# The stage ahead of the latent attentions: a rope moved across a stage boundary, keys of two heads in one product, an early exponential table, an output by banks

## The reference, cut to what matters

```
h = x normed, times w_in_2        -> q, k_cmp, v_cmp, k_sel, v_sel, k_win, v_win, gates, cq, ckv, kr
sparse attention: k_cmp, v_cmp compressed by a small MLP to 31 blocks (silu);
  softmax over the blocks, over the selected and over the window keys, summed with the gates
latent attention: q = norm(cq) w_q_up, [k, v] = norm(ckv) w_kv_up, kr shared by 8 heads
x = x + [sparse, latent] w_out ;  x = x + relu(norm(x) w_ff1)^2 w_ff2
```

## Time and profile before

| what | value |
|---|---|
| time, 3 runs | median 2813.57 us (2811.67 to 2826.16) |
| profiled execution, own time | 2809.47 us |
| its span | 2807.7 us |
| mean granted PE clock over the span | 0.961 |
| PE busy | 2617.4 us (93% of the span) |
| prepare stage, first layer | PE from 1530.03 to 1583.21 us |
| prepare stage, second layer | PE from 2206.19 to 2259.21 us |

### The profile page before, as it was taken

The page is one execution under the profiler, slowest core; times in us unless marked ns, Lnnn a source line. Parts: engine busy times, 40 slices in busy tenths (PEclk is TensorE's granted clock), DMA queues, the critical chain, the costliest instruction groups (busy, mean ns, idle before and its releaser), DMA issues. The chain is left out here.

```text
span 2807.7 us, 56794 instructions
## 1 busy us (share of the span) xinstructions
PE 2617.4 (93%) x21851; PEld 1768.2 (63%) x21852; DVE 1350.4 (48%) x2758; ACT 747.9 (27%) x1650; POOL 301.1 (11%) x449
## 2 busy tenths in 40 slices
PE   6999889899988889998979999999999999999998
PEld 6977774344433333443457567888888666888887
DVE  3246645344433434454465675533344576543333
ACT  4235430000000000000032565422233256433222
POOL 4121002122222112222210000000000000000000
PEclk8999999999999999999989999999999999999999
DMA  7353169999999999899973201222223300122221
GB/s 226 87 210 116 76 261 380 420 418 405 419 420 403 419 419 411 340 418 419 416 267 101 91 2 37 91 91 98 90 101 91 112 31 1 68 91 98 90 95 56
DMA packets 170890, 588.47 MB, mean 210 GB/s; under 512 B 28238, under 2 KB 55694, under 8 KB 121512
## 3 DMA queue, kind: packets, MB, share of 16 engines
q1 hardware_dynamic: 158112, 562.91, 51.2%
q0 software_dynamic: 10192, 18.09, 1.9%
q10 hardware_dynamic: 2360, 4.29, 0.4%
HBM read 573.54 MB, written 17.45 MB: 210 GB/s over the span
## 5 line engine op out<-in xcount | busy, mean ns | idle before, releaser
L2774 PE MATMUL moe_up<-expert_w,mod 128*32 128x512 f32 x3200 | 395.2, 620 | 52.5 <-DMA expert_w<-in_exp_w_up 26.7
L2774 PEld LDWEIGHTS moe_up<-expert_w,mod 128*32 128x32 f32 x3200 | 114.2, 112 | 283.4 <-issue 213.5
L2839 ACT ACTIVATE mod<-mod 128x256 f32<-128x256 f32 x85 | 35.5, 417 | 965.2 <-DVE mod L2875 956.4
L2774 PE MATMUL moe_up<-ring,mod 128*32 128x512 f32 x1784 | 219.3, 612 | 26.8 <-DMA ring<-in_exp_w_up 20.5
L423 ACT ACTIVATE feed_w<-ring 128x1024 fp32r<-128x1024 f32 (+1 forms) x160 | 153.8, 1035 | 263.5 <-PE feed_bank L370 263.5
L2783 PE MATMUL moe_down<-expert_w,mod 128*32 128x256 f32 x3568 | 216.5, 386 | 1.7 <-DVE mod L2886 1.7
L368 PE MATMUL feed_bank<-feed_w,mlp_u_hi 128*128 128x512 f32 x512 | 199.3, 389 | 0.0
L370 PE MATMUL feed_bank<-feed_w,mlp_u_lo 128*128 128x512 f32 x512 | 199.2, 389 | 0.0
L369 PE MATMUL feed_bank<-feed_w,mlp_u_hi 128*128 128x512 f32 x512 | 199.2, 389 | 0.0
L2783 PEld LDWEIGHTS moe_down<-expert_w,mod 128*32 128x32 f32 x3568 | 132.6, 112 | 96.4 <-issue 42.1
L437 DVE TENSOR_TENSOR feed_w<-ring,feed_w 128x1024 fp32r<-128x1024 f32 (+1 forms) x160 | 185.4, 1221 | 13.2 <-ACT feed_w L423 12.9
(11 more groups left out here) (556 smaller groups left out, 5035.3 us busy)
## 6 DMA issues: line engine op xcount, KB each, us to landing
expert_w<-in_exp_w_up SPq DMA_DIRECT2D x153, 1024.0 KB, 10.4
expert_w<-in_exp_w_down SPq DMA_DIRECT2D x83, 1024.0 KB, 10.3
ring<-in_exp_w_up SPq DMA_DIRECT2D x80, 1024.0 KB, 10.4
ring<-in_w_ff SPq DMA_DIRECT2D x32, 2048.0 KB, 8.8
ring<-in_exp_w_down SPq DMA_DIRECT2D x32, 1024.0 KB, 10.2
ring<-in_ada_w SPq DMA_DIRECT2D x12, 2048.0 KB, 10.5
x<-in_exp_w_up SPq DMA_DIRECT2D x23, 1024.0 KB, 10.3
x<-in_exp_w_down SPq DMA_DIRECT2D x13, 1024.0 KB, 10.0
```

The costliest lines, as they stand in the source:

```text
L2774: mm = nc.tensor.matmul(up[quarter[q], :], rowsT[:, c, :], w[:, q], start=(c == 0), stop=(c == UPS - 1))
L2839: nc.scalar.activation(sig, gate, ACT.Sigmoid, scale=ALPHA).then_inc(sig_ready, 1)
```

## The change

- Rope of the keys: tiles 0 and 1 after job 13 as before, tile 2 after job 14 (when ACT has copied job 14), tile 3 no longer in the projection's stage: its four instructions stand at the head of DVE's list in the prepare stage, with `rot[:, 0]` as room, and PE waits for the last of them ahead of the transposes of `k_cmp`.
- Key columns of all heads first, then the value columns, in `w_kv_up_2` (set in order on the host ahead of the launch). A key up now makes two heads in one product with 128 weight columns: 4 key ups in place of 8, 16 ups in all. Each is copied out by two copies of 64 partitions.
- An exponential of one column (`warm`) right after the silu on ACT.
- `ov` is laid out so that a bank holds one group and two tiles; PE signals after each bank, and DVE multiplies bank by bank, four instructions in place of two.

```diff
-        if n in (13, 15):
-            dve.wait_ge(self.evac_done["act"], self.before["act"] + (n + 1) // 2)
-            dve.wait_ge(self.evac_done["dve"], self.before["dve"] + (n + 1) // 2)
-            for t in (n - 13, n - 12):
+        if n in (13, 14):
+            dve.wait_ge(self.evac_done["act"], self.before["act"] + n // 2 + 1)
+            dve.wait_ge(self.evac_done["dve"], self.before["dve"] + 7)
+            for t in {13: (0, 1), 14: (2,)}[n]:
...
+        warm = sb("warm", [P, 1])
...
-        ov = ctx.enter_context(nc.psum_tensor(f"prep{l}_o", [P, NT, COL], F32))
+        ov = ctx.enter_context(nc.psum_tensor(f"prep{l}_o", [P, 2 * G2, 2, 256], F32))
...
-        wv = wkv[:, 0, :].rearrange("p (h n) -> p h n", n=DN + DV2)[:, :, DN:]
+        wv = wkv[:, 0, H2 * DN:]
...
-        ups = [("q", *j) for j in UPQ] + [("v", t) for t in range(NT)] + [("k", h) for h in range(H2)]
+        ups = [("q", *j) for j in UPQ] + [("v", t) for t in range(NT)] + [("k", h) for h in range(0, H2, 2)]
...
-                    c = job[1] * (DN + DV2)
-                    mm = nc.tensor.matmul(out[:DN, :], wkv[:, 0, c:c + DN], lat[:, 2, :], start=True, stop=True)
+                    mm = nc.tensor.matmul(out, wkv[:, 0, job[1] * DN:(job[1] + 2) * DN], lat[:, 2, :], start=True, stop=True)
...
             pe.wait_ge(lat_dve, 1)
+            pe.wait_ge(key_added, 1)
             turn(bank[1], columns_of(tok, KC, P)).then_inc(kc_turned, 1)
...
-            for n in range(12, 15):
+            for n in range(12, 14):
...
-            for n in range(15, 20):
+            for n in range(14, 16):
...
-                    pe.wait_ge((up_act, up_dve)[h % 2], 9 + h // 2)
+                    pe.wait_ge((up_act, up_dve)[h % 2], 7 + h // 2)
...
-                    mm = nc.tensor.matmul(ov[:, t, g * 256:(g + 1) * 256], pT[:, g, t * P:(t + 1) * P], vbd[:, g, :], start=True, stop=True)
-                mm.then_inc(valued, 1)
+                    mm = nc.tensor.matmul(ov[:, 2 * g + t // 2, t % 2, :], pT[:, g, t * P:(t + 1) * P], vbd[:, g, :], start=True, stop=True)
+                    if t % 2:
+                        mm.then_inc(valued, 1)
...
+            return [(mkT[0:DN, job[1] + m, :], src[m * DN:(m + 1) * DN, :]) for m in range(2)]
...
             nc.scalar.activation(hid[:], bank[0][:, 0:CHID], ACT.Silu).then_inc(activated, 1)
-            for n in (8, 10, 12, 14):
+            nc.scalar.activation(warm[:], k.eps[:], ACT.Exp)
+            for n in (8, 10, 12):
                 take_up(n)
...
-            for n in (16, 18):
-                take_up(n)
+            take_up(14)
...
+            nc.vector.tensor_tensor(other[..., 0:w], keys[..., w:], ksin[..., 0:w], ALU.mult).then_inc(key_turned, 1)
+            nc.vector.tensor_tensor(other[..., w:], keys[..., 0:w], ksin[..., w:], ALU.mult).then_inc(key_turned, 1)
+            dve.wait_ge(key_turned, 2)
+            nc.vector.tensor_tensor(keys, keys, kcos, ALU.mult).then_inc(key_turned, 1)
+            dve.wait_ge(key_turned, 3)
+            nc.vector.tensor_tensor(keys, keys, other, ALU.add).then_inc(key_added, 1)
             dve.wait_ge(lat_turned, 2)
...
-            dve.wait_ge(valued, G2)
-            for g in range(G2):
+            for b in range(2 * G2):
+                g, ts = b // 2, slice(b % 2 * 2, b % 2 * 2 + 2)
+                dve.wait_ge(valued, b + 1)
```

More of the change, by code:

```diff
@@ L3140, in prepare_stage @@
         paired, placed = sem("paired"), sem("placed")
+        key_turned, key_added = sem("key_turned"), sem("key_added")
         kr_turned, kr_spread = sem("kr_turned"), sem("kr_spread")
@@ L3147, in prepare_stage @@
             sem(t) for t in ("biased", "shifted", "raised", "weighed", "ca_turned", "ca_taken", "valued", "step"))
-        ov = ctx.enter_context(nc.psum_tensor(f"prep{l}_o", [P, NT, COL], F32))
+        ov = ctx.enter_context(nc.psum_tensor(f"prep{l}_o", [P, 2 * G2, 2, 256], F32))
         low = [ctx.enter_context(nc.psum_tensor(f"prep{l}_bank{i}", [P, COL], F32)) for i in range(4)]
-        bank = [b[:] for b in low] + [ov[:, t, :] for t in range(NT)]
+        bank = [b[:] for b in low] + [ov[:, b].rearrange("p t n -> p (t n)") for b in range(2 * G2)]
         w1 = [chunk_view(k, ("cmp", l, kv))[0] for kv in "kv"]
         wq, wkv = chunk_view(k, ("up", l))
-        wv = wkv[:, 0, :].rearrange("p (h n) -> p h n", n=DN + DV2)[:, :, DN:]
+        wv = wkv[:, 0, H2 * DN:]
         block = ctx.enter_context(nc.Block())
@@ L3277, in up_out @@
             if job[0] == "q":
-                return tok[:, job[1], job[2]:job[3]], src[:, 0:job[3] - job[2]]
-            return (mv[:, job[1], :], src) if job[0] == "v" else (mkT[0:DN, job[1], :], src[:DN, :])
+                return [(tok[:, job[1], job[2]:job[3]], src[:, 0:job[3] - job[2]])]
+            if job[0] == "v":
+                return [(mv[:, job[1], :], src)]
+            return [(mkT[0:DN, job[1] + m, :], src[m * DN:(m + 1) * DN, :]) for m in range(2)]
         @block.scalar
@@ L3284, in take_up @@
                 act.wait_ge(upped, n + 1)
-                nc.scalar.activation(*up_out(n), ACT.Copy).then_inc(up_act, 1)
+                for dst, src in up_out(n):
+                    copied = nc.scalar.activation(dst, src, ACT.Copy)
+                copied.then_inc(up_act, 1)
             for i, gain in ((0, k.q_norm[:, l, 0:1]), (2, k.kv_norm[:, l, :])):
@@ L3336, in take_up @@
                 dve.wait_ge(upped, n + 1)
-                nc.vector.tensor_copy(*up_out(n)).then_inc(up_dve, 1)
+                for dst, src in up_out(n):
+                    copied = nc.vector.tensor_copy(dst, src)
+                copied.then_inc(up_dve, 1)
             def pair_up(i, b, turns):
@@ L3372, in _ @@
             dve.wait_ge(up_dve, 4)
+            dve.wait_ge(key_added, 1)
             nc.vector.tensor_tensor(rot[:, :, :, 0:DR // 2], q[:, :, :, DR // 2:], sn[:, :, :, 0:DR // 2], ALU.mult).then_inc(rot_turned, 1)
@@ L3393, in _ @@
                     nc.vector.tensor_copy(vbd[32 * r:32 * r + 32, g, 64 * r:64 * r + 64], bank[g][32 * r:32 * r + 32, 0:DK2]).then_inc(vbd_made, 1)
-            for n in (15, 17, 19):
-                take_up(n)
+            take_up(15)
             dve.wait_ge(k.groups_done, up_done)
@@ L3720, with keys_then_values @@
           "w_q_up_2 mla_kv_norm_2 w_kv_up_2 nsa_out_norm_2 mla_out_norm_2 w_out_2 mlp_norm_2 w_ff1_2 w_ff2_2 final_norm_2").split()
+def keys_then_values(w):
+    heads = w.reshape(*w.shape[:2], H2, DN + DV2)
+    return np.ascontiguousarray(np.concatenate([heads[..., c].reshape(*w.shape[:2], -1) for c in (slice(0, DN), slice(DN, None))], axis=-1))
 def kernel(**inputs):
@@ L3728 @@
     arrays = {n: np.ascontiguousarray(inputs[n]) for n in INPUTS}
+    arrays["w_kv_up_2"] = keys_then_values(arrays["w_kv_up_2"])
     arrays |= {f"const_{n}": v for n, v in host_constants().items()}
```

9 lines of the change are left out of this document (6 added, 3 removed).

## The result

The changed kernel takes 2784.62 us (median of 4 runs, 2783.47 to 2788.04), the kernel before in 4 runs 2812.62 us (2805.29 to 2826.16): ratio 0.9897, with a 95% interval of 0.9858 to 0.9936. The forecast was 2787.5 us, faster, range 2780 to 2799.

A forecast was written before the change was run, and what follows sets the result against it. PE was taken as the bound in the dense stretch, with DVE, ACT and a halved clock costing time at the stage's edges. Six terms sum to 13.05 us a layer, 26.1 for two: 2787.5 us as median, range 2780 to 2799.

The forecast's parts named there:

- 1. Rope: Projection's end to prepare stage: with the turns moved, SP arrives last and PE begins earlier, saving 2.7 us a layer.
- 2. The clock behind it: Start of the prepare stage: the clock stays up, so 28 transposes take 0.109 us each instead of 0.211; 2.8 us a layer.
- the nearest row: Profile row from 1575 to 1579 us: PE had a 1.46 us gap and the clock stayed at 1.00.
- the clock falls at the first boundary too: Rival, both boundaries at low clock: gain only 8.65 us a layer, 2796.3 us in all; chance 0.12.
- The thin cover of 0.4 us for `kv_up`: Before the ups: `kv_up` lands at 1531.7 us, PE asks for the up weights at 1532.1.
- late weights: Rival at the ups: small loads served before `kv_up` make PE wait 1.7 us a layer, 2790.9 us; chance 0.05.
- 3. Keys of two heads: Key ups in the prepare stage: four products fewer, eight records at 0.434 us, save 3.5 us a layer of full PE.
- 4. The table: Load before the exponential moves behind silu, so the mask begins earlier: 0.8 us a layer, bounds 0 and 1.28.
- 5. Output by banks: End of the prepare stage: only one 0.69 us multiplication of 2.35 remains behind PE's last bank; 1.65 us a layer.
- 6. The clock in the attention: Attention's start: idle time falls from 2.77 to 1.1 us, the clock stays up; 1.6 us a layer, bounds 0 and 2.4.
- the largest rival (0.30): Attention's start stays at half clock: gain 11.45 us a layer, 2790.7 us in all; chance 0.30.
- The side "slower": Clock stays low beyond the transposes, in the always-busy stretch from 1536 to 1572 us; 2832 us if all slow; chance 0.02.

The follow-up runs named there:

- table alone: Only the one-column exponential behind silu, put on the kernel before; one execution, 2805.01 us beside 2805.86.
- rope alone: Only the moves of tile 2's and tile 3's key rope, put on the kernel before; one execution, 2797.49 us beside 2809.68.
- the kernels whose gaps were filled: Unread PE products added in idle time: kernel before with 24 and 14, 2802.77 us; with 11 and 6, 2799.5; changed kernel with fills, 2781.06.

## Why the prediction was right, point by point

**1. Rope, 2.7 us: right.** 2.71 measured (2.65 in the second layer), with SP's drain the last to arrive. No cover was used up: the rope of tile 3 ends at 1529.68 and the copy behind it at 1530.34, 2.5 and 1.9 us ahead of the transposes that need them.

**2. The clock behind it, 2.8 us: right, and the nearest row was the right one.** 2.82 in the first layer, 2.66 in the second. The rival "the clock falls at the first boundary too" did not happen in any of 10 stages with a gap of 1.35 us. The bound behind it was near, though: at 2.61 and 2.56 us it fell, twice out of twice. The length of one gap would not have been enough everywhere: at the attention's end, behind gaps of 1.61, 1.03 and 2.01 us close together, the clock falls. The thin cover of 0.4 us for `kv_up` held; PE goes from its transposes to the ups without a wait, although the small loads issued behind the boundary landed after 3.9 to 4.5 us instead of 2.1: the part of the rival "late weights" that was true, but it reached no waiting instruction. The transfers issued from 1525 to 1536 us in the changed kernel (KB, us to landing):

```profile
prep_w2k<-in_cmp_w_k SPq DMA_DIRECT2D x2, 64.0 KB, 4.5
prep_w2v<-in_cmp_w_v SPq DMA_DIRECT2D x1, 64.0 KB, 3.9
```

**3. Keys of two heads, 3.5 us: the mechanism was right, the term too small by 0.4.** 3.87 measured, in every kernel that has the edit. The sixteen records of the key ups took 2.72 + 4.44 = 7.16 us up to what follows them, 0.4475 each, so eight fewer are 3.58; the 0.434 of the working runs from the first start to the last and leaves out the step behind the last record. The other 0.29 us the working had as unchanged: 0.2 in the small products between and 0.1 in the step to the first key up. No cover failed.

**4. The table, 0.8 us: right.** 0.80 and 0.80 alone. The Trainium skill, ScalarE: Activation LUTs, What ACT_TABLE_LOAD costs, gives some 1.38 us of drain behind the load, and the trace again does not agree: from the end of the load at 1552.82 the next ACTIVATE takes 0.01 us to begin, and PE's way to the scores did not grow by the 0.3 us that would follow (12.49 us with the table alone).

**5. Output by banks, 1.65 us: right in size, 1.74, but by a thinner cover than I said.** The one piece of 0.69 us behind PE's last bank is what was taken; the inverse sums, however, were ready only at 1571.76, 0.6 us behind the first bank, and three multiplications of together 2.04 us stand between them and the last one. Of the 2.2 us up to the end of the last bank 0.17 were left, where the working had 1.2 to spare. Later by more than that, and the term would have begun to shrink.

**6. The clock in the attention, 1.6 us: right.** 1.67 and 1.65. This was the term with the largest rival (0.30). With 1.03 us of gap the clock stayed up in all 12 stages that had it. At the old gap of 2.77 us the rival's case is open each time: with rope alone and with table alone it fell in one layer and held in the other.

**The sum.** 13.05 us a layer was forecast, 13.59 and 13.03 were measured. That the second layer met the sum is luck: 0.4 us too little in item 3 stands against 0.35 that the clock behind the scores takes back and 0.14 of item 2. The two layers together gained 0.5 us more than forecast, and the match of the whole (2783.47 for 2783.4) came about since 0.6 us outside of the stage went the other way: 0.9 us longer ahead of it, 0.3 shorter behind. Such parts differ from execution to execution; the last product of the first layer's projection ends anywhere from 1521.5 to 1527.6 us in the twelve profiled ones. The side "slower" named a low clock in the dense stretch and gave it 0.02, deciding from 17.3 us of it a layer. That very thing did appear, where PE is busy without a pause, but for some 3.4 us in one of the two layers, at a cost of 0.3 us: the argument "against it" in the prediction, that a low stretch ended when PE had worked without a pause, told when the clock comes back, not that it cannot fall while PE is busy. That step was wrong, and it cost nothing worth naming here. In the kernels whose gaps were filled it cost 0.3 to 1.7 us a fall, and 0.94 with rope alone.

## What to carry to other kernels

Read the granted clock behind every gap of a matrix engine before pricing the gap: here 4.06 us of idle time cost another 2.82 us, so that half of what the moved rope brought was clock, and leaving one tile of it at its old place would have given back more than its own length. Where the work that makes the gap cannot be moved, idle products in it do the same for the clock, as long as they end ahead of the real last arrival and PE is the one that the others wait for behind it. Look at what lies ahead of the gap as well: several short gaps in a row cost the clock here as one long gap did. And a chain that ends a stage is worth cutting by banks even when its links are nearly in step, since only the last piece counts.

## What the runs showed of the hardware that was not expected

- At the two edges of the prepare stage, with PE busy nearly without a pause just ahead of the gap (4.34 of 4.50 us before, 4.87 of 5.10 in the changed kernel, ahead of the attention), the clock never fell behind gaps of 1.03 us (12 stages), 1.35 (10), 1.43 (2), 1.54 and 1.60; behind 2.61 and 2.56 it fell both times, at a cost of 1.67 us; behind 2.77 it fell in full in 4 of 8 attentions, in part in 2 and not at all in 2; behind 4.00 and 4.06 it fell in all 8 stages, at 1.7 to 2.9 us. The Trainium skill, TensorE: Matmul & The Clock Gate, What you observe, says of the step to the faster pace under steady work that it varies from run to run. The traces agree: behind gaps of 4.00 and 4.06 us the clock came back 3.6 to 6.0 us after the first transpose. That the fall as well may come or not behind the same 2.77 us is what these runs show.
- Behind gaps of 1.61, 1.03 and 2.01 to 2.12 us close together, with PE busy for 3.69 of 8.2 us, it fell in 22 of 22 places.
- The clock also fell while PE was busy without a pause, in or behind the scores (64 products of 32 columns, 3.69 us): 8 of 12 stages that had begun at 1.00, 2 of 2 with the products made twice (9.76 and 8.64 us for 7.4), and none of 10 stages that had begun at 0.50.
- A product of f32 with 128 moved columns stands as two records and takes about 0.23 us (24 of them 5.52), while a transpose of the same size is one record and takes 0.109.
